# The order of TensorE's products in the attention projections and four recurrence groups of a two-layer decoder trunk

## The reference, cut to what matters

```
u = rms_norm(h) @ w_in                  # layer 0: split into a_val, a_gate, xr, gr
xr = causal_depthwise_conv(xr, 4 taps)
r, i = sigmoid(per-head xr @ w_a + b), sigmoid(per-head xr @ w_x + b)
yb = scan(a(r), sqrt(1 - a^2) * i * xr) * gelu(gr)

q, k, v = split(rms_norm(h) @ w_qkv)    # layer 1
z = q k^T / sqrt(128)
log_w = log_sigmoid(z) + suffix sums of (-softplus(z)) over later keys
out = exp(log_w), masked, @ v
```

## Time and profile before

| | |
|---|---|
| median of 3 runs | 2369.76 us (2368.81 to 2373.4) |
| the profiled execution's own time | 2369.46 us |
| its span, first to last instruction | 2367.6 us |
| TensorE busy | 2329.2 us, 98% of the span |
| VectorE busy | 1544.4 us, 65% |
| ScalarE busy | 1253.0 us, 53% |
| mean granted TensorE clock | 0.997 of full speed |
| HBM | 428.05 MB read, 182 GB/s over the span |

### The profile page before, as it was taken

One profiled execution on the slowest core, in us unless ns is written; L12 is line 12 of the kernel. 1 busy time (PEld: TensorE's weight loads), 2 busy tenths in 40 slices (PEclk: granted clock), 3 DMA queues, 4 the chain that ended last, 5 costly groups with the idle time before them and its releaser, 6 DMA issues.

```text
span 2367.6 us, 39239 instructions
## 1 busy us (share of the span) xinstructions
PE 2329.2 (98%) x13706; PEld 2067.3 (87%) x13706; DVE 1544.4 (65%) x1882; ACT 1253.0 (53%) x1600; POOL 22.7 (1%) x31
## 2 busy tenths in 40 slices
PE   7999999999999999999999999999999999999997
PEld 6888998888888888888888888888888888888886
DVE  7789886556556556677766766765555555556676
ACT  6676565445435435555566666554444444445554
POOL 0001000000000000000000000000000000000000
PEclk9999999999999999999999999999999999999998
DMA  7669865655655655665655555566556556556553
GB/s 240 208 151 208 210 202 172 194 188 185 198 185 183 194 190 181 196 190 178 194 179 161 177 156 177 177 193 194 178 194 196 177 192 198 177 191 199 177 176 109
DMA packets 440763, 439.59 MB, mean 186 GB/s; under 512 B 13552, under 2 KB 438640, under 8 KB 440688
## 3 DMA queue, kind: packets, MB, share of 16 engines
q1 hardware_dynamic: 431952, 429.97, 57.4%
q0 software_dynamic: 8448, 8.39, 2.5%
q10 hardware_dynamic: 288, 0.23, 0.0%
HBM read 428.05 MB, written 2.10 MB: 182 GB/s over the span
## 4 chain that ended last, share of the span: by engine, by line
PE 88%; DVE 4%; DMA 4%; ACT 2%; issue 1%; DVEq 0%; SPq 0%; ACTq 0%
PE ps L447 53%; PE ps L453 27%; PE ps L445 2%; DMA spl<-raw 1%; DVE spl L1199 1%; PE ps L452 1%; DMA raw<-in_w_out 1%; ACT spl L773 1%; PE ps L488 1%; PE ps L490 1%; PE ps L489 1%; DMA raw<-in_w_in 1%; DVE y L1603 0%; DMA raw<-in_w_o 0%; PE O L609 0%
## 5 line engine op out<-in xcount | busy, mean ns | idle before, releaser
L1199 DVE TENSOR_TENSOR spl<-raw,spl 128x1024 fp32r<-128x1024 f32 x794 | 933.7, 1221 | 578.9 <-ACT spl L773 572.6
L773 ACT ACTIVATE spl<-raw 128x1024 fp32r<-128x1024 f32 x826 | 832.4, 1055 | 701.4 <-PE ps L453 601.5
L447 PE MATMUL ps<-XA,spl 128*128 128x512 f32 x3072 | 787.2, 393 | 16.5 <-DVE spl L1199 10.1
L447 PE MATMUL ps<-XB,spl 128*128 128x512 f32 x2784 | 711.5, 392 | 0.0
L447 PEld LDWEIGHTS ps<-XA,spl 128*128 128x128 f32 x3072 | 544.7, 189 | 102.1 <-issue 11.2
L447 PEld LDWEIGHTS ps<-XB,spl 128*128 128x128 f32 x2784 | 491.4, 188 | 75.5
L453 PEld LDWEIGHTS ps<-XA,spl 128*128 128x128 f32 x3072 | 435.4, 191 | 42.9
L453 PE MATMUL ps<-XA,spl 128*128 128x256 f32 x3072 | 444.2, 282 | 0.0
L453 PEld LDWEIGHTS ps<-XB,spl 128*128 128x128 f32 x2784 | 394.5, 191 | 39.0
L453 PE MATMUL ps<-XB,spl 128*128 128x256 f32 x2784 | 402.6, 281 | 0.0
L1235 DVE TENSOR_TENSOR tv<-cross,ps 128x512 f32<-128x512 f32 x189 | 128.7, 681 | 9.4 <-ACT cross L773 9.1
(11 more groups left out here) (181 smaller groups left out, 1232.7 us busy)
## 6 DMA issues: line engine op xcount, KB each, us to landing
raw<-in_w_up SPq DMA_DIRECT2D x256, 512.0 KB, 4.8
raw<-in_w_down SPq DMA_DIRECT2D x256, 512.0 KB, 5.2
raw<-in_w_qkv SPq DMA_DIRECT2D x96, 512.0 KB, 4.5
raw<-in_w_in SPq DMA_DIRECT2D x64, 512.0 KB, 4.9
raw<-in_w_gate SPq DMA_DIRECT2D x64, 512.0 KB, 4.6
raw<-in_w_out SPq DMA_DIRECT2D x32, 512.0 KB, 4.9
raw<-in_w_o SPq DMA_DIRECT2D x32, 512.0 KB, 4.6
spl<-raw POOLq DMA_DIRECT2D x16, 512.0 KB, 6.3
```

The lines of the kernel that those rows point to most:

```text
L447: pe.matmul(ps[:, b + o, :], w[:, q, 0, c], x[:, kt, :, :], start=start, stop=False)
L773: return act.activation(out, in_, ACT.Copy, scale=scale)
L1199: dve.tensor_tensor(s[:, :, 1, :], raw[:, m % NRAW, :, :], s[:, :, 0, :].bitcast(F32), ALU.subtract).then_inc(lo_ready, 1)
```

## The change

`whole` takes two more arguments: `tokens_out`, handed on to its products, and `mid`, which is called once, between its hi and its lo phase. The four recurrence groups G_REC+4 to G_REC+7 and the attention groups outside the first pair's q and k (three for each of 7 pairs and one for the first, 22 in all) go from `gemm` to `whole`. `suffix_sums` and `values` then stand between the phases. The number and shapes of all products stay. ACT, DVE, SP and POOL keep their code and order.

```
-            def whole(g, gi, m, it, x, tiles=None):
+            def whole(g, gi, m, it, x, tiles=None, tokens_out=False, mid=None):
...
                     for q in range(4):
                         for o in range(2):
-                            hi_product(b, m + j, q, o, x, 4 * j + q, j == 0 and q == 0, False)
+                            hi_product(b, m + j, q, o, x, 4 * j + q, j == 0 and q == 0, tokens_out)
+                if mid is not None:
+                    mid()
                 for j in range(4):
                     lo_there(pe, m + j, it)
                     for q in range(4):
                         for o in range(2):
-                            mm = lo_product(b, m + j, q, o, x, 4 * j + q, j == 3 and q == 3, False)
+                            mm = lo_product(b, m + j, q, o, x, 4 * j + q, j == 3 and q == 3, tokens_out)
                     mm.then_inc(chunk_used, 1)
...
-            gemm(G_REC + 4, 0, C_REC + 16, 0, XA)
+            whole(G_REC + 4, 0, C_REC + 16, 0, XA)
...
-            gemm(G_REC + 5, 0, C_REC + 20, 0, XA)
+            whole(G_REC + 5, 0, C_REC + 20, 0, XA)
...
-            gemm(G_REC + 6, 0, C_REC + 24, 0, XA)
+            whole(G_REC + 6, 0, C_REC + 24, 0, XA)
...
-            gemm(G_REC + 7, 0, C_REC + 28, 0, XA)
+            whole(G_REC + 7, 0, C_REC + 28, 0, XA)
...
-                    gemm(g, i * 6, m, i * 3, XB)
-                    gemm(g + 1, i * 6, m + 4, i * 3, XB, mid=lambda: suffix_sums(s - 1, i))
-                gemm(g + 2, i * 6, m + 8, i * 3, XB, tokens_out=True,
-                     mid=None if first else lambda: values(s - 1, i, (s - 1) % 2))
+                    whole(g, i * 6, m, i * 3, XB)
+                    whole(g + 1, i * 6, m + 4, i * 3, XB, mid=lambda: suffix_sums(s - 1, i))
+                whole(g + 2, i * 6, m + 8, i * 3, XB, tokens_out=True,
+                      mid=None if first else lambda: values(s - 1, i, (s - 1) % 2))
```

## The result

| | before | after |
|---|---|---|
| median of 4 runs | 2369.49 us (2368.81 to 2373.4) | 2400.62 us (2398.07 to 2404.76) |
| ratio | | 1.013, 95% interval 1.0115 to 1.0145 |
| profiled execution, its span | 2369.46, 2367.6 us | 2398.07, 2396.3 us |
| mean granted clock | 0.997 | 0.991 |

The four runs of before are the three of the table further up and one more. The change made the kernel 31 us (1.3%) slower. Slower was forecast, but 17 us of it, and the measured time lies outside the range of 2376 to 2397.

What follows compares the result with a forecast made beforehand. TensorE's own products were taken to bound the kernel. Attention waits 14.7 us, less 0.7 for the order, plus 3.2 in the recurrence gave 17.2 us on 2369.46, so 2386.7 us; range 2376 to 2397.

Steps and rivals of the forecast that it cites:

- What bounds the kernel: In the changed stages TensorE's products set the end; the chain between `suffix_sums` and `values` must finish before TensorE needs it.
- Part 1, the order itself: In 26 groups of attention and recurrence, the `whole` form gains 0.03 us a group, 0.8 us in all.
- Part 2, the chain: In attention, later chunk releases delay the weights; TensorE waits 2.13 us at `values` in seven pairs, 14.7 us net.
- a pair pays once and nothing is carried over: In attention, each pair's wait at `values` shifts everything behind it equally; nothing else in the next pair is late.
- Part 3, the recurrence: Group 7's late splits make TensorE wait 2.9 us at `rg_head(3, 0)`; ACT's chain makes the whole 3.2 us late.
- the wait near 138.5, named as a sign: In the recurrence, TensorE's wait on `tv` near 138.5 was to show the forecast right.
- TensorE's clock: Behind the 2.1 us waits at `values` no clock fall was assumed; one fall was priced at 1.6 us.
- the clock falls after each wait: Rival: the clock falls behind each of seven attention waits, 11.0 us more, giving 2397.9 us; chance 9%.

Runs made afterwards that it cites:

- fitted kernel: Changed kernel with ACT's and DVE's steps in attention's part 1 and the recurrence's last pair moved ahead of late splits; 2370.52 us, ratio 1.0006.
- part 1 alone: Kernel before with only attention's part 1 groups in the `whole` form, attention's parts 0 and 2 and the recurrence in `gemm`; 2415.66 us, ratio 1.0195.
- `values` a chunk later: Changed kernel with `values` called after the lo products of the first chunk of attention's part 2; 2381.46 us, ratio 1.0057.
- the recurrence alone changed: Kernel before with only the four recurrence groups in the `whole` form, attention as before; 2372.48 us, ratio 1.0016.
- part 1 as before: Changed kernel with only attention's part 1 groups back in `gemm`; 2373.04 us, ratio 1.0013.
- groups 4 to 6 alone: Kernel before with only recurrence groups 4, 5 and 6 in the `whole` form, group 7 and attention as before; 2370.22 us, ratio 1.0003.
- the smaller filling: Changed kernel with 6 extra products ahead of the wait for the attention weights in each pair but the last; 2388.26 us, ratio 1.0082.
- the filled wait: Changed kernel with 14 extra products ahead of the wait for the attention weights in each pair but the last; 2388.22 us, ratio 1.0076.
- values at the end: Changed kernel with `values` of the pair before at the end of attention's part 2, ahead of `scores`; 2374.77 us, ratio 1.0028.
- attention-only kernel: Kernel before with only the attention groups in the `whole` form, the recurrence groups in `gemm`; 2395.23 us, ratio 1.0113.

## Why the prediction was wrong

- *What bounds the kernel* held: TensorE did, and the chain from the suffix sums to `values` was what could stop it.
- *Part 1, the order itself*: forecast 0.03 us a group. The fitted kernel shows (37.35 - 37.21) / 3 = 0.05 in one trace. Right in sign and without weight.
- *Part 2, the chain*: cut at 12.94 and rest's end at 21.52 forecast, 12.93 and 21.52 measured. Waits of 2.13 forecast, 2.1 to 2.2 measured (1.9 where the trace says "issue"). The experiments with part 1 alone (3.8 us) and with `values` a chunk later (1.0 to 1.2) moved the wait as the working says. The statement that a pair pays once and nothing is carried over held within attention. It left out its end: the per-layer embedding's products waited 1.3 us (for ACT's `pp`) in place of 0.3, which is 1 us. The reading that TensorE waits only in the first 360 us or at the ends had passed over this place: the kernel before waits there too, 0.33 us at 1451 and 0.87 at 1482.
- *Part 3, the recurrence*: 2.9 us forecast and 2.7 measured for the wait, 3.2 against 3.5 in the trace and 2.9 in the medians for the whole. Group 7 was needed for the wait, as said. The clock fell behind the 2.7 us (0.50 over 3.40 us), and that cost nothing of its own, as the working had it: with the recurrence alone changed it did not fall there, and TensorE then waited 1.30 us for `tv` at 138.69; in the changed kernel the fall used that time up and the wait near 138.5, named as a sign, did not come.
- *TensorE's clock* is the step that failed. "I take no fall for those of 2.1, which are nearest to 1.90." The clock fell behind all seven in the profiled execution, and each fall lost 1.65 to 1.7 us: 7 x 1.65 = 11.6 us. With it and the 1 us the sum is 17.2 + 11.6 + 1 = 29.8, for 28.6 in the profiled execution and 31 in the medians. The slower runs of the changed kernel have the lower clocks: 2398.07 and 2398.78 us at 0.991 and 0.992, 2402.46 at 0.990, 2404.76 at 0.988.
- The rival "the clock falls after each wait" gave 2397.9 us, the time of the profiled execution within 0.2, and it had 9%. (Its line has 11.0 for 7 x 1.6, which is 11.2; the 2397.9 holds the 11.2. That it meets the profiled time so closely is in part luck, since the 1 us at the end of attention, the 1.5 us at the start and the smaller waits weigh against each other.) The Trainium skill's sentence on re-throttling in each pass of a loop ("TensorE: Matmul & The Clock Gate", section "HAM oscillation — how this bites in real kernels") stood beside it. Its example has waits for DMA of some 3 to 5 us in each pass; here waits of 1.9 to 2.2 us did the same (0.50 behind them), and the measurement decides. I had two rows to set between, a gap of 1.9 us without a fall and one of 3.3 with one, and the new gaps lay between. Two points don't make a threshold, and the price of the falls, 11 us in the sum, was nearly that of the waits themselves. The range ended at 2397, below the rival's own 2397.9. In hindsight I would give the rival a third of the chance and let the range reach 2405.

## What to carry to other kernels

When a group of products gives back its buffers later, find what stands behind the refill in the in-order queues of the other engines: here the cut, the exp and the mask stood behind splits that nobody was in a hurry for, and moving them ahead took away 26 us of loss. When TensorE is the bound and a change gives it a wait of about 2 us in a loop, price each wait twice, with and without the half clock behind it, and give both real chances. Where the wait can't be removed, moving part of TensorE's own work into it, or even products whose results are thrown away, kept the clock here.

## What the hardware showed that I had not expected

- Waits of about the same length did and did not bring the clock down. The wait for `xrp` near 37 us was followed by a half clock at 2.5 us (with part 1 as before, and with groups 4 to 6 alone) and not at 2.1 or 2.4 us (the changed and the fitted kernel). The wait of 2.7 us at `rg_head(3, 0)` brought the clock down in four of seven traces (the changed kernel, part 1 as before, the smaller filling, values one chunk later) and left it at 1.00 in three (only the recurrence, the filled wait, values at the end). A wait near 240 us did so at 2.2 us (groups 4 to 6 alone) and not at 2.4 (values one chunk later). So the length of a wait alone does not decide; what does is open. The first `values` wait of 2.1 us left the clock alone in the attention-only kernel, and each of the next six brought it down. The windows behind the first and the second of them:

```profile
1214.00:1217.40 3.40, 3.40 (x30) 3.40 (x31) 1.75 (x3) 1.47 (x2) 0.00 (x0) 1.00 0.49 154
1254.40:1257.80 3.40, 3.40 (x18) 3.40 (x18) 0.82 (x2) 1.08 (x2) 0.00 (x0) 0.51 0.32 111
```

- Waits of 1.0 to 1.3 us at `values` never brought it down, in 14 cases.
- Two kernels that differ by 98 useless products run at 2388.2 and 2400.6 us, and the one with the more products is the faster.
- By the pairs' lengths, a wait of 3.8 us cost about 3.1 us beside itself (44.2 - 37.35 - 3.7), one of 2.1 us 1.65.
